# Norms between two layers taken by token halves, late modulation groups in their own buffer, and the opening stage re-ordered

## What is computed

```python
for i in range(2):
    shift, scale, gate = split(c @ ada_w[i] + ada_b[i], 3)           # per sequence
    h = rmsnorm(x, norm_pre[i]) * (1 + scale) + shift
    if i == 0:
        y, S, last = rwkv7_time_mix(h, ...)    # mixes h with the token before: xm[mu] = h + xx*mu, 6 mu's
    else:
        c_kv, k_pe = shared_kv(x, c, ...)      # rmsnorm(x, kv_norm)*(1+scale)+shift, @ kv_w_a, norm, rope
        qg = h @ w_in                          # 384 columns of q latent, 1024 of gate
        q = rmsnorm(qg[:384]) @ w_q            # then attention over c_kv, k_pe
        y = (attention * silu(qg[384:])) @ w_out
    x = x + gate * rmsnorm(y, norm_post[i])
```

## Time and profile before

| | us |
|---|---|
| three runs, lowest / median / highest | 1095.7 / 1099.76 / 1102.14 |
| the profiled execution, its own time | 1100.46 |
| its span, first to last instruction | 1098.4 |
| PE busy | 1016.0 (93%) |
| DVE busy | 485.3 (44%) |
| ACT busy | 333.6 (30%) |
| POOL busy | 96.1 (9%) |

### The profile page before, as it was taken

One profiled execution on the slowest core, in us unless ns is written; L12 is line 12 of the kernel. 1 busy time (PEld: TensorE's weight loads), 2 busy tenths in 40 slices (PEclk: granted clock), 3 DMA queues, 4 the chain that ended last, 5 costly groups with the idle time before them and its releaser, 6 DMA issues.

```text
span 1098.4 us, 23985 instructions
## 1 busy us (share of the span) xinstructions
PE 1016.0 (93%) x10615; PEld 714.9 (65%) x10615; DVE 485.3 (44%) x927; ACT 333.6 (30%) x634; POOL 96.1 (9%) x140
## 2 busy tenths in 40 slices
PE   2887999999999999999899898999899999999996
PEld 1465777777676777777554345888684766666566
DVE  2874344463645445363554956211102444544105
ACT  2313322423332332323311325222323444444102
POOL 1002001110100011010100320000010001100111
PEclk9988999999999999999999898999899899999988
DMA  9502022030403122040232767120224222523002
GB/s 383 213 2 77 2 81 80 11 149 2 158 2 100 61 79 81 2 158 3 98 144 79 272 245 291 54 91 29 101 80 95 78 97 97 188 102 116 39 1 78
DMA packets 20135, 110.33 MB, mean 100 GB/s; under 512 B 7224, under 2 KB 11968, under 8 KB 13888
## 3 DMA queue, kind: packets, MB, share of 16 engines
q1 hardware_dynamic: 13136, 84.41, 20.6%
q0 software_dynamic: 2304, 20.97, 5.3%
q10 hardware_dynamic: 4592, 3.42, 1.0%
HBM read 102.27 MB, written 5.19 MB: 98 GB/s over the span
## 4 chain that ended last, share of the span: by engine, by line
PE 82%; DVE 10%; ACT 3%; issue 3%; DMA 2%; ACTq 0%; SPq 0%; DVEq 0%
PE pj L987 20%; PE pj L1465 7%; PE pj L1376 6%; PE pj L1516 3%; PE pj L1227 3%; PE pj L1394 3%; PE bk L1097 2%; PE bk L1568 2%; PE bk L1103 2%; PE bk L1496 2%; PE bk L1110 2%; DVE XM L1823 2%; PE bk L914 2%; PE bk L1552 2%; PE bk L1553 2%
## 5 line engine op out<-in xcount | busy, mean ns | idle before, releaser
L987 PE MATMUL pj<-XM,ring 128*128 128x260 f32 x992 | 253.1, 395 | 6.3 <-DVE R L1873 4.7
L987 PEld LDWEIGHTS pj<-XM,ring 128*128 128x128 f32 x992 | 178.7, 191 | 43.2 <-issue 11.9
L1465 PE MATMUL pj<-XM,ring 128*128 128x260 f32 x352 | 79.4, 388 | 2.9 <-ACT XM L799 2.9
L1465 PEld LDWEIGHTS pj<-XM,ring 128*128 128x128 f32 x352 | 67.7, 193 | 14.3 <-issue 3.8
L1933 DVE TENSOR_TENSOR arena<-arena,bk 128x512 f32<-128x512 f32 x40 | 27.5, 688 | 76.4 <-PE bk L1110 76.4
L661 ACT ACTIVATE ring<-bk 128x512 f32<-128x512 f32 x40 | 23.9, 598 | 106.9 <-PE bk L1103 106.6
L1928 DVE TENSOR_TENSOR arena<-bk,arena 128x512 f32<-128x512 f32 x40 | 27.7, 692 | 42.9 <-PE bk L1097 42.9
L855 ACT ACTIVATE arena<-bk,arena 128x128 f32<-128x128 f32 (+3 forms) x32 | 16.9, 528 | 76.0 <-DVE arena L2185 50.5
L1227 PE MATMUL pj<-R,ring 128*128 128x512 f32 x64 | 33.9, 645 | 5.7 <-DVE R L1985 4.2
L1906 DVE TENSOR_TENSOR ring<-bk,arena 128x512 f32<-128x512 f32 x32 | 22.0, 689 | 36.4 <-PE bk L1052 35.9
L1516 PE MATMUL pj<-arena,ring 128*128 128x260 f32 x144 | 34.8, 408 | 0.0
(11 more groups left out here) (359 smaller groups left out, 1786.1 us busy)
## 6 DMA issues: line engine op xcount, KB each, us to landing
ring<-in_ada SPq DMA_DIRECT2D x14, 2048.0 KB, 8.7
ring<-in_w_in SPq DMA_DIRECT2D x8, 2048.0 KB, 7.4
ring<-in_b_w_in SPq DMA_DIRECT2D x3, 2048.0 KB, 11.6
XM<-in_ada SPq DMA_DIRECT2D x2, 2048.0 KB, 24.6
ring<-in_w_out SPq DMA_DIRECT2D x2, 2048.0 KB, 7.9
R<-in_xT SPq DMA_DIRECT2D x2, 1040.0 KB, 6.5
R<-in_xT SPq DMA_DIRECT2D x1, 2080.0 KB, 13.7
XM<-in_Sd SPq DMA_DIRECT2D x1, 2048.0 KB, 18.5
```

The lines of the kernel that those rows point to most:

```text
L987: last = mm(out, w[:, e, k, :], XM[:, e, k, a * HALF:(a + 1) * HALF], start=(k == 0), stop=(k == KT - 1))
L1465: last = mm(pj[:, t % 2, a, 0:HALF], w[:, k, e * P:(e + 1) * P], H1[:, k, a * HALF:(a + 1) * HALF], start=(k == 0), stop=(k == KT - 1))
```

## The change

- **Opening**: all six constants are issued by SP ahead of x, `shiftT` and `lora1` by SP between the second and the third `ada` group; the masks stay on ACT's queue. `ada` groups three and four go to slots 0 and 1 of XM, so that the lora mixes (mu 4 and 5) go to slots 2 and 3 and are followed by mu 0 and 1; mu 3 and 2 come last in each half. PE's order is hidden, e = 0, e = 1, (second half: `lora(0)`), e = 3. `project(0, 0)` still waits for all four groups to be added by DVE, which now comes after 16 mixes instead of 12.
- **Handover**: tiles 4 to 7 of the output product by halves of tokens (256 and 264 columns with the decode ones); square sums, residual, second norm and layer input by halves as well, with the input product of layer 1 cut into 11 + 11 half tiles and the work of the second half between those of the first. `H1` lies in R1, the scale is folded into one DVE instruction, only the shift is ACT's. Decode columns are summed with the second half. `HK` and the five 4096-column DVE steps of the decode state come under the input product, the state's store on SP after the kv weights.
- **Late ada groups**: each in XM slot 2 (`latew`) with its own semaphore, one load after the other; the ring carries only the nine other loads.
- **Attention**: `row_values(n-1)` after `cache_scores(n-1)` in step n, instead of `row_values(n)` at the end of step n; DVE's `gate_head` after `decode_max`. `gather_latents(0)` on POOL waits for the end of the input product.

```diff
+            for name, dst in (("ones", ones[:, :]), ("cT", cT[:, :, :]), ("sel", sel[:, :]), ("vecs", vecs[:, :, :]),
+                              ("adab", adab[:, :]), ("ident", ident[:, :])):
+                sp.dma_start(dst, d[name]).then_inc(s_const, 16)
             for i in range(2):
                 sp.dma_start(R0[:, 4 * i:4 * i + 4, :], d["xT"][:, 4 * i:4 * i + 4, :]).then_inc(s_x[i], 16)
             for i, g in enumerate(FIRST):
+                if i == 2:
+                    sp.dma_start(shin, d["shiftT"]).then_inc(s_l1, 16)
+                    sp.dma_start(lora1, d["lora1"]).then_inc(s_l1, 16)
                 sp.dma_start(adaw[i], d["ada"][g]).then_inc(s_ada[i], 16)
...
-            for n in (5, 3, 4, *range(6, len(stream))):
-                sp.wait_ge(*used(n - 3))
+            for i in range(1, NADA):
+                sp.wait_ge(s_wu, i)
+                late_group(i)
+                if i < 3:
+                    sp.wait_ge(*used(i - 1))
+                    load(i + 2)
+            for n in range(5, len(stream)):
+                sp.wait_ge(*used((3, 4, 2, 5)[n - 5]))
                 load(n)
-                if n == 3:
+                if n == 5:
                     sp.wait_ge(s_dd, 3)
                     sp.dma_start(o["wkv_s"], Sd).then_inc(s_dso, 16)
...
             for half in range(2):
                 lora_hidden(half)
-                for e in (3, 0, 1):
+                for e in (0, 1):
                     project(0, e, 4 * half, 4 * half + 4)
-            lora(0)
-            pe.wait_ge(s_g0, 1)
+                if half:
+                    lora(0)
+                project(0, 3, 4 * half, 4 * half + 4)
             head_sums(0, 0)
...
+            ada(0)
+            early_part(28, 32)
+            first_part(0, 4)
+            ada_turn(0)
+            for t in range(5, KT):
+                first_part(0, t)
+            pe.wait_ge(s_ydm, 32)
+            tr(bk[:, 3, 0:HD], ydt[0:HD, :], ident[0:HD, 0:HD]).then_inc(s_ydt, 1)
+            ada(1)
+            output_sums(0)
+            first_part(1, 4)
+            ada_turn(1)
+            pe.wait_ge(s_r1, 1)
+            first_rows(0)
+            first_rows(1)
+            first_part(1, 5)
+            turn_first_rows()
+            residual_sums(0)
+            first_part(1, 6)
+            first_part(1, 7)
+            ada(2)
+            output_sums(1)
+            b_in(0, 0)
+            ada_turn(2)
+            for t in range(1, 4):
+                b_in(0, t)
+            residual_sums(1)
+            ada(3)
+            b_in(0, 4)
+            ada_turn(3)
+            for t in range(5, BT):
+                b_in(0, t)
+            pe.wait_ge(s_hh, 1)
+            for t in range(BT):
+                b_in(1, t)
...
+            residual(0)
+            scales(A1, M_SC1, V_PRE1)
+            normed_input(0)
+            residual(1)
+            gate(0, 0)
+            normed_input(1)
+            for t in range(1, KT):
+                gate(0, t)
+                if t in (3, 5):
+                    state_step(t // 2 - 1)
+            for n in (2, 3, 4):
+                state_step(n)
+            gate(1, 0)
...
                 if n >= 1:
                     cache_scores(n - 1)
+                if n >= 1:
+                    row_values(n - 1)
                 if s >= 1 and g == 2:
                     turn_weights(s - 1)
                 turn_rows(n)
                 turn_cache(n)
                 if s >= 1 and g == 3:
                     decode_values(s - 1)
-                row_values(n)
             cache_scores(NSTEP - 1)
+            row_values(NSTEP - 1)
```

More of the change, by code:

```diff
@@ new lines, in _ @@
+            b_in(0, 1)
+            residual_squares(1, 4, 7)
+            b_in(0, 2)
+            residual_squares(1, 7, KT)
+            b_in(0, 3)
+            rstd(st[:, HALVES[1]])
+            ada_rows(3)
+            b_in(0, 4)
+            shifted(1, 0, 4)
+            b_in(0, 5)
+            shifted(1, 4, KT)
+            b_in(0, 6)
+            ada_tiles(3)
+            for t in range(7, BT):
+                b_in(0, t)
+            for t in range(BT):
+                b_in(1, t)
+                if t == QT:
+                    rstd(st2)
+                    act.dma_start(UV, d["uv"]).then_inc(s_uv, 16)
@@ L1470, in _ @@
+            pe.wait_ge(s_hh, 1)
+            for t in range(BT):
+                b_in(1, t)
                 if t == QT:
-                    pe.wait_ge(s_nq, NQ_O1)
+                    pe.wait_ge(s_nd, 4)
+                    pe.wait_ge(s_qq, 2 * QT)
                     for k in range(QT):
@@ L1733, in add_squares @@
                     then(G.tensor_tensor(x[:, 0, c], x[:, 0, c], x[:, t, c], ALU.add), s_acc)
[L1735 removed]
+            for t in range(1, KT - 1):
+                pool.wait_ge(s_nq, t + 1)
+                then(G.tensor_tensor(SQ[:, 0, HALVES[0]], SQ[:, 0, HALVES[0]], SQ[:, t, HALVES[0]], ALU.add), s_acc)
+            pool.wait_ge(s_nq, NQ_ROWS)
+            for t in range(1, KT - 1):
+                if t == KT - 2:
+                    pool.wait_ge(s_nq, NQ_ROWS + 1)
+                then(G.tensor_tensor(SQ[:, 0, HALVES[1]], SQ[:, 0, HALVES[1]], SQ[:, t, HALVES[1]], ALU.add), s_acc)
             then(G.memset(kpeZ[ROPE:P, 0, :], 0.0))
@@ new lines, in kv_input @@
+            def kv_input(k0, k1):
+                if k0 == 0:
+                    dve.wait_ge(s_adb, ADA_MT * NADA)
+                    scales(A2, M_SCK, V_KVN)
+                for k in range(k0, k1):
+                    x = HK[:, k, 0:T]
+                    then(V.scalar_tensor_tensor(x, R0[:, k, 0:T], A2[:, k, 0:1], st[:, 0:T], ALU.mult, ALU.mult))
+                    mark(V.tensor_scalar(x, x, mod[:, M_SHK + k, 0:1], None, ALU.add))
+                if k1 == KT:
+                    x = HK[:, :, T:N]
+                    then(V.tensor_tensor(x, R0[:, :, T:N], std, ALU.mult))
+                    then(V.tensor_tensor(x, x, A2[:, :, 1:9], ALU.mult))
+                    then(V.tensor_tensor(x, x, mod[:, M_SHK:M_SHK + KT, 1:9], ALU.add), s_hh)
@@ new lines, in gate @@
+            def gate(i, t):
+                v, c = BT * i + QT + t, HALVES[i]
+                dve.wait_ge(s_ba, v + 1)
+                then(V.tensor_tensor(GATE[:, t, c], GATE[:, t, c], pj[:, v // 2 % 2, v % 2, 0:c.stop - c.start], ALU.mult), s_bd)
+            then(V.tensor_tensor(A0[:, :, :], mod[:, M_G0:M_G0 + KT, :], b9(vecs[:, V_POST0, :]), ALU.mult))
+            residual(0)
[3 more added lines that the diff above has]
+            gate(0, 0)
@@ L2149, in _ @@
+            for t in range(1, KT):
+                gate(1, t)
+                if t == 1:
+                    kv_input(0, 4)
+                if t == 3:
+                    kv_input(4, KT)
+                if t == 5:
+                    dve.wait_ge(s_na, nn[0])
+                    then(V.tensor_tensor(qa, qa, st2.unsqueeze(1).to_broadcast([P, QT, N]), ALU.mult))
                     for k in range(QT):
@@ L2243, in _ @@
                 s, g = n // TT, n % TT
-                if s >= 1 and g == 0:
-                    gate_head(s - 1)
                 if n + 1 < NSTEP:
```

417 lines of the change are left out of this document (206 added, 211 removed).

## The result

The changed kernel takes 1068.36 us (median of four executions, 1066.41 to 1070.97) against 1097.85 for the kernel before, run beside it on the same chip: ratio 0.9728, 95% interval 0.9686 to 0.977. Six more executions beside other runs gave 0.9742 (0.9713 to 0.9771). The forecast was 1076.7 us with a range of 1067 to 1087: the direction and the range held, and the forecast's middle was 8.3 us too high. The profiled execution took 1066.41 us, its span 1064.6; PE is busy for 996.8 us of it (94%).

A forecast was written before the change was run, and what follows sets the result against it. PE, busy 93% of the span, was taken as the bound, so gains are its lost waits: opening 10, handover 12.8, attention 1.0, sum 23.8 us. From 1100.5 that gives 1076.7 us, range 1067 to 1087.

The forecast's parts named there:

- Opening, 10 us: Opening: earlier loads, hidden product at full clock and gate product under the chain gain 10 us, bounds 6 to 13.
- The order of the loads: Opening: PE starts 3.6 us earlier and loses a 0.9 us wait, so the first mix comes at 35.15 us.
- the bounds: Opening: 6 (loads late by 2 us, low clock) to 13 us (ada products already at 1.90 us, first load at once).
- the 11 us: Opening: gain if the second hidden product runs at full clock (3.7 us); 8.4 if it stays at the low clock.
- The gate product under the chain: Opening: e = 3, 3.6 us, moves under the 9.2 us chain from lora(0) to "ss", which still sets the end.
- Handover, 12.8 us: Handover: waits, slow residual sums, slow first input tile and small decode sums go, 12.8 us, bounds 7 to 15.
- Just in time for `b_in(0, 0)`: Handover: H1 by T + 46 and ACT's shift by T + 51, against b_in(0, 0) at T + 51.5.
- the low bound of 7: Handover: gain of only 7 us if halves cost DVE as much as wholes and a late group comes late by 3.
- a late group: Handover: a late ada group arriving 3 us late, part of the low bound; group one was forecast T + 20, needed T + 23.
- GpSimd's adds: Handover: six second-half adds beside DVE's second norm end by T + 47, nothing charged; slow adds a rival, chance 0.05, 1085.
- Attention, 1.0 us: Attention: 7.4 us of waits before row_values go, 5.6 at cache_scores and 0.75 for gate_head come; bounds 7.4 gained, 4 lost.
- more than forecast: Rival, chance 0.08: no exposed waits at cache_scores in attention and a faster second ada product in the opening give 1068 us.

The follow-up runs named there:

- the two experiments: Kernel before with only the changed opening: 1088.1 us, ratio 0.9907; changed kernel with the old opening put back: 1080.77 us, ratio 0.9813.
- open_back: Changed kernel with the whole opening put back (constants, ada slots, order of mixes and products): 1080.77 us, ratio 0.9813 to the kernel before.
- lora_late: Changed kernel with lora(0) behind the second half of the gate product e = 3: 1073.8 us, ratio 0.9783 to the kernel before.
- rows_back: Changed kernel with row_values and gate_head put back where they stood before: 1073.21 us, ratio 0.9767 to the kernel before.
- best: Changed kernel with row_values ahead of cache_scores and the last kv turn behind the first q output tile: 1059.53 us, ratio 0.9642 to the kernel before.

## Why the prediction was right, and what was mis-sized

- **Opening, 10 us: right, in part by luck.** 10.4 and 9.3 us by the two experiments (7.8 against the changed kernel's second ratio). PE's first product came at 16.22 (forecast 16.0), the second hidden product at 57.31 for 3.73 us (58.6, 3.7), e = 1's end at 68.29 (69.5). Two terms were off and nearly cancel. The order of the loads is worth 6.0 us at the first mix in this profile and not 4.5 (33.68, forecast 35.15), since the second `ada` product took 1.91 us, which stood among the bounds. The 2.7 us for the hidden product at full clock, counted in the 11 us, `open_back` shows without the change. Loads and gate product alone, 6.0 + 3.6, make 9.6, and even this varies: the second hidden product starts between 56.4 and 59.6 in the profiles with the new opening. By the two profiles alone it would have been 14.1 us at T, but T varies: 593.87 to 596.52 in the profiles of kernels whose opening is the changed one, 607.96 and 606.05 with the old one.
- **The gate product under the chain: right.** `lora_late` shows the chain's price, 2.1 us at the start of `project(0, 2)`.
- **Handover, 12.8 us: right in place and size.** T to the kv tiles is 139.2 to 140.2 us in the eleven profiles with the new handover, 151.7 and 152.9 in the two with the old one: 11.4 to 13.7. The milestones lie within 1 us of the forecast's (`residual_sums(0)` T + 38.4 for 38, `b_in(0, 0)` 51.8 for 51.5, `b_in(0, 4)` 72.0 for 71). The kv tiles come at T + 139.5 for 138. "Just in time for `b_in(0, 0)`" holds for the end of the chain (ACT's shift ends at T + 51.3), but there is slack ahead of it: DVE's residual ends at 627.7 and ACT's last four squares begin at 632.67, behind the decode rows. So 3.4 us more of DVE cost nothing, and that part of the low bound of 7 was too cautious; a late group, its other part, was not tried.
- **GpSimd's adds: right to charge nothing, for a half-right reason.** Five of the six take 0.74 us because they end before DVE's second norm begins; the sixth meets it and takes 0.99, so they do contend. They end at T + 47.1, as forecast (T + 47).
- **Attention, 1.0 us: mis-sized, the one part that was.** It measured 3 to 5 us by the stage, 4.5 at the same clock (4.3 to 4.9 by the times, 2.7 against the second ratio). The step "Net 7.4 - 5.6 - 0.75 = 1.0 us gained" added up waits from the list, and these came as forecast (7.4 against 5.8 and 0.8, eight of 0.7). It failed in two ways. The 7.4 is too small for what goes: by the start times the waits before `row_values` cost 10.8 us in `rows_back`, where the list has 7.6, while the new ones are listed nearly in full. And it took PE's own time to be the same in either order, where the transpositions are 1.7 us shorter behind `row_values`.
- **The rest of the 8.3 us.** 2.6 us are the start: the sum was made against a profiled execution of 1100.46 us, and the median beside the changed kernel is 1097.85. The other 5.7 are gain, 29.5 against 23.8. Attention is about 3.5 of them (4.5 for 1.0); the last 2 us are no more than the two medians of the changed kernel differ by (1068.36 and 1070.72), and no step can be named for them.

The rival "more than forecast" (1068) gave the time, but through another cause: its faster `ada` product came, its missing exposure in attention did not.

## What to carry to other kernels

A move inside a loop is not costed by the list of waits alone. Compare the times from start to start: a wait of 0.20 us in the list delayed PE by 0.36 here, some were not listed, and an instruction takes longer behind one neighbour than behind another. A few hundredths or tenths of a microsecond per step were most of this gain. Before you add up two traces, look for a stretch that differs although the change doesn't touch it (here the q products), and take it out of the sum. A wait that precedes a long stretch of products costs more than it lasts in some executions, and an independent product put into it takes the wait away. Five executions of that kernel lay within 2.3 us, but the six of `best` spread over 4.9 again, so a smaller spread is not shown.

## What was not expected of the hardware

- Behind the same wait of 2.98 us the granted clock fell to its lower level (0.50 for five microseconds) in six profiles of eleven and stayed at the higher one in five, at 3 us a time. In the two profiles with 0.35 us of wait it did not fall.
- `project(0, 2)` behind "ss": 7.28 us in seven of ten profiles with a wait of 2.0 us and 8.97 in the other three; 8.8 to 10.0 in all three with a wait of 4.7 to 4.8.
- GpSimd's adds doubled DVE's two-input instructions that ran beside them, from 0.48 to 0.96 to 0.98 us each, and took 0.82 instead of 0.74 themselves; the one add that meets DVE in the changed kernel took 0.99.
- A constant of 64 KB landed 17.0 us after its issue on ACT's queue, beside two loads of 2 MB, and 2.2 us after it on SP's queue ahead of them.
- The first transposition behind the small cache products (8 rows) took 0.165 us from start to start, behind `row_values` (128 rows) 0.11.
